# Modulation sums shared between VectorE and GpSimd, and the first block's stages on one calendar of row blocks

## What is computed

```python
def first_block(x, ...):
    h = rms_norm(x, norm_gain)
    proj = einsum('bsd,dc->bsc', h, w_in)                    # 1024 x 10240
    sb_q, sb_k, sb_v, sb_g, r_q, r_k, r_v, r_g, m_sb, m_ret = split(proj)
    out_a = stick_breaking_attention(rms_norm(sb_q), rms_norm(sb_k), sb_v) * silu(sb_g)   # 8 heads of 128
    out_b = rms_norm(chunkwise_retention(rotary(r_q), rotary(r_k), r_v)) * silu(r_g)      # 4 heads of 256
    merged = sigmoid(m_sb + b0) * (out_a @ w_branch_sb) + sigmoid(m_ret + b1) * (out_b @ w_branch_ret)
    return x + merged @ w_out

def second_block(x, c, ...):
    mod = silu(c) @ w_ada + b_ada            # 1024 x 6144, one row: shifts, scales and gates
    sh1, sc1, gt1, sh2, sc2, gt2 = split(mod, 6)
    h = rms_norm(x, norm_mix) * (1 + sc1) + sh1
    x = x + gt1 * token_mixer(h, ...)        # latent attention and an RWKV-7 branch
    h = rms_norm(x, norm_ffn) * (1 + sc2) + sh2
    return x + gt2 * peer_ffn(h, ...)        # 16384 experts
```

## Time and profile before

| | us |
|---|---|
| median of 3 runs | 1748.14 |
| lowest, highest | 1744.11, 1757.19 |
| the profiled execution, its own time | 1747.92 |
| its span in the trace | 1746.6 |
| TensorE busy | 1639.4 (94%) |
| VectorE busy | 889.7 (51%) |
| GpSimd busy | 415.9 (24%) |
| mean granted TensorE clock | 0.969 of full |

### The profile page before, as it was taken

One profiled execution on the slowest core, in us unless ns is written; L12 is line 12 of the kernel. 1 busy time (PEld: TensorE's weight loads), 2 busy tenths in 40 slices (PEclk: granted clock), 3 DMA queues, 4 the chain that ended last, 5 costly groups with the idle time before them and its releaser, 6 DMA issues.

```text
span 1746.6 us, 24304 instructions
## 1 busy us (share of the span) xinstructions
PE 1639.4 (94%) x9529; PEld 1215.1 (70%) x9529; DVE 889.7 (51%) x1838; ACT 545.1 (31%) x929; POOL 415.9 (24%) x273
## 2 busy tenths in 40 slices
PE   6998999999989996788889999999999999999998
PEld 2333554554445544754779999999999988888886
DVE  4775223331225326453458886333333477767776
ACT  1002333120112213111124344443334444545553
POOL 0000000000000021000048888888888200000000
PEclk9999999999999986989899999999999999999999
DMA  9993334233463473012346666666677477777776
GB/s 343 350 327 135 134 107 145 96 110 139 148 219 108 145 296 137 3 49 98 133 146 149 146 146 139 142 144 146 144 140 142 108 240 240 241 240 240 240 238 214
DMA packets 179572, 297.17 MB, mean 170 GB/s; under 512 B 48786, under 2 KB 94210, under 8 KB 179332
## 3 DMA queue, kind: packets, MB, share of 16 engines
q1 hardware_dynamic: 110704, 260.28, 43.6%
q0 software_dynamic: 36864, 0.15, 6.1%
q10 hardware_dynamic: 31892, 35.20, 5.9%
HBM read 276.55 MB, written 19.03 MB: 169 GB/s over the span
## 4 chain that ended last, share of the span: by engine, by line
PE 86%; DVE 7%; DMA 3%; issue 2%; ACT 2%; POOL 0%; ACTq 0%; SPq 0%; DVEq 0%; POOLq 0%
PE bank L456 26%; PE bank L869 14%; PE bank L867 14%; PE bank L871 13%; PE bank L879 6%; PE bank L849 3%; DVE ada_acc L964 3%; DMA slot<-in_w_in_dram 1%; PE bank L725 1%; PE bank L440 1%; DMA ada_b<-in_b_ada_dram 1%; DMA slot<-in_expert_down_dram 1%; PE bank L736 1%; PE bank L473 1%; PE bank L735 0%
## 5 line engine op out<-in xcount | busy, mean ns | idle before, releaser
L456 PE MATMUL bank<-slot,hT 128*128 128x512 f32 (+2 forms) x1088 | 479.6, 596 | 14.1 <-DMA slot<-in_w_in_dram 9.7
L1979 POOL DMA_INDIRECT c_dram<-gates,places x256 | 397.7, 1553 | 201.4 <-DVE gates L1512 123.7
L456 PEld LDWEIGHTS bank<-slot,hT 128*128 128x128 f32 x1088 | 206.7, 194 | 255.5 <-issue 244.3
L867 PE MATMUL bank<-hT_high,dT_high 128*128 128x256 f32 x1024 | 297.6, 291 | 0.0
L869 PE MATMUL bank<-hT_low,dT_high 128*128 128x256 f32 x1024 | 287.8, 281 | 0.0
L871 PE MATMUL bank<-hT_high,dT_low 128*128 128x256 f32 x1024 | 287.6, 281 | 0.0
L1424 DVE TENSOR_TENSOR dT_low<-bank,dT_high 128x512 fp32r<-128x512 f32 x256 | 165.0, 686 | 218.7 <-ACT dT_high L1900 217.5
L869 PE MATMUL bank<-up_low,A_high 128*128 128x512 f32 x512 | 202.2, 395 | 0.0
L867 PE MATMUL bank<-up_high,A_high 128*128 128x512 f32 x512 | 199.6, 390 | 0.4 <-DVE A_low L1424 0.4
L871 PE MATMUL bank<-up_high,A_low 128*128 128x512 f32 x512 | 198.8, 388 | 0.0
L867 PEld LDWEIGHTS bank<-hT_high,dT_high 128*128 128x128 f32 x1024 | 193.8, 189 | 0.0
(11 more groups left out here) (394 smaller groups left out, 1717.5 us busy)
## 6 DMA issues: line engine op xcount, KB each, us to landing
slot<-in_expert_down_dram SPq DMA_DIRECT2D x128, 512.0 KB
slot<-in_expert_up_dram SPq DMA_DIRECT2D x128, 512.0 KB, 3.4
slot<-in_w_in_dram SPq DMA_DIRECT2D x27, 2048.0 KB, 8.0
P<-in_w_ada_dram ACTq DMA_DIRECT2D x24, 1024.0 KB
c_dram<-zeros SPq DMA_DIRECT2D x1, 16384.0 KB, 50.7
slot<-c_dram SPq DMA_DIRECT2D x128, 128.0 KB, 3.3
slot<-in_w_out_dram SPq DMA_DIRECT2D x4, 2048.0 KB, 7.9
slot<-in_w_query_dram SPq DMA_DIRECT2D x4, 2048.0 KB, 8.1
```

Source lines behind the costliest of these rows:

```text
L456: m = pe.matmul(sums, lhsT=lhs[:, k, t * P:(t + 1) * P], rhs=w[:, k, :], start=(k == 0), stop=(k == w.shape[1] - 1))
L867: pe.matmul(o, lhsT=lhs_high.bitcast(F32R), rhs=rhs_high.bitcast(F32R), start=start, stop=False, skip_group_check=True)
L1979: g.indirect_dma_start(C_dram, bass.IndirectOffsetOnAxis(ap=places[:, x, k:k + 1], axis=0), gates[:, x, k:k + 1], None, compute_op=ALU.add ...
```

## The change

The 24 pieces are divided. VectorE sums pieces 0 to 11 as before, one at each of x = 2 to 13. GpSimd (`g_ada`) takes the other twelve: one product of all eight slices with the broadcast column `cs`, then additions of the halves (1024, 512 and 256 columns). Each engine has two weight buffers (RQ, RK for VectorE; M1, M2 for GpSimd). Two pieces share one row product of 512 columns, so that TensorE makes 12 of them, at x = 4, 5, 6, 8, 9, 10, 12, 13, 15, 16, 20 and 23, and biases and results are moved as 12 rows of 512. The loads of the pieces and biases move from ScalarE's queue to SyncE's, between the chunks; the constants are loaded by ScalarE's queue at once. One loop over x now orders every engine: a pair of attention heads starts at x = 14, 18, 22, 26 and takes six steps (normalise, transpose, scores, VectorE's part of the scores, running sums, weighting); the retention pairs start at x = 30 and 34; the square sums stand at x = 8 to 13 and the gates' silu at x = 17 and 33. ScalarE does each function for both heads of a pair in a row. `oaT` is transposed ahead of the block x = 39. The diff, cut:

```diff
--- before.py
+++ after.py
-    NP, AW, PIECES = 6, 256, ((0, 1), (2,), (3, 4), (5,))
-    ada_in = [sem(f"ada{p}_in") for p in range(NP)]
-    mod_out = [sem(f"mod_out{p}") for p in range(NP)]
-    ada_summed = sem("ada_summed")
+    AW = 256
+    SB, RET = [14 + 4 * i for i in range(4)], [30, 34]
+    ADA = 6 * D // AW // 2
+    ada_at = {2 + p: p for p in range(ADA)}
+    rows = [(4, 0, 0), (5, 1, 0), (6, 0, 1), (8, 0, 2), (9, 1, 1), (10, 0, 3), (12, 1, 2), (13, 0, 4), (15, 0, 5),
+            (16, 1, 3), (20, 1, 4), (23, 1, 5)]
+    row_at = {x: (n, who, m) for n, (x, who, m) in enumerate(rows)}
+    pool_load = {int((11.8 * (p - 1) + 4) / 6.9) + 1: p for p in range(2, ADA)}
+    row_of = {(who, m): n for n, (x, who, m) in enumerate(rows)}
+    ada_in = [[sem(f"ada{who}{j}_in") for j in range(2)] for who in ("v", "g")]
+    ada_b_in = [sem(f"ada_b{j}_in") for j in range(2)]
+    mod_out = [sem(f"mod_out{j}") for j in range(2)]
+    ada_summed = [sem("ada_summed_v"), sem("ada_summed_g")]
...
-    ada_w = [P1[:, p // 3, RQ + 2 * (p % 3):RQ + 2 * (p % 3) + 2, :].rearrange("p g d -> p (g d)")
-             .rearrange("p (k n) -> p k n", k=KT) for p in range(NP)]
-    ada_acc = [carve(f"ada_acc{p}", AW) for p in range(NP)]
-    ada_b = [carve(f"ada_b{p}", AW) for p in range(NP)]
-    mod_row = [carve(f"mod_row{p}", AW) for p in range(NP)]
+    ada_w = [[P1[:, j, at:at + 2, :].rearrange("p g d -> p (g d)").rearrange("p (k n) -> p k n", k=KT) for j in range(2)]
+             for at in (RQ, M1)]
...
+    ada_acc = [[gt[:, j * 2 * AW:(j + 1) * 2 * AW] for j in range(2)], [carve(f"ada_acc{j}", 2 * AW) for j in range(2)]]
+    cursor[0] = ret_at
+    ada_b = [carve(f"ada_b{j}", 2 * AW) for j in range(2)]
+    mod_row = [carve(f"mod_row{j}", 2 * AW) for j in range(2)]
...
+    def pe_ada_row(x):
+        if x in row_at:
+            n, who, m = row_at[x]
+            row = fill(("ada", n), 4 + n % 2)[0:1, :]
+            pe.wait_ge(ada_summed[who], 2 * m + 2)
+            pe.matmul(row, lhsT=col[:, 0:1], rhs=ada_acc[who][m % 2], start=True, stop=True).then_inc(filled(("ada", n)), 1)
...
+        for x in range(40):
+            for i in range(4):
...
+                step = {1: pe_sb_turn, 2: pe_sb_score, 4: pe_sb_keep, 5: pe_sb_weigh}.get(x - SB[i])
+                if step == pe_sb_turn and i == 0:
+                    pe.wait_ge(first_in, 16 * 9)
...
+                step = {2: pe_ret_turn, 3: pe_ret_score, 4: pe_ret_weigh}.get(x - RET[i])
...
+            if x == 39:
+                for j in range(2):
+                    clear(pe, ("sbo", 3, j))
+                pe_turn("oaT", tiles_of(P1[:, :, G_, :]))
+            pe_block(("in", x // 2), hT, x % 2)
+            pe_ada_row(x)
...
+    def v_ada_sum(x):
+        if x in ada_at:
+            p = ada_at[x]
+            m = p // 2
+            acc, w = ada_acc[0][m % 2][:, p % 2 * AW:(p % 2 + 1) * AW], ada_w[0][p % 2]
+            v.wait_ge(ada_in[0][p % 2], 16 * (m + 1))
+            if m > 1:
+                held(v, ("ada", row_of[0, m - 2]))
+            v_own.settle(v.tensor_scalar(acc, w[:, 0, :], cs[:, 0:1], None, ALU.mult))
             for k in range(1, KT):
-                m = v.scalar_tensor_tensor(ada_acc[p], ada_w[p][:, k, :], cs[:, k:k + 1], ada_acc[p], ALU.mult, ALU.add)
+                m = v.scalar_tensor_tensor(acc, w[:, k, :], cs[:, k:k + 1], acc, ALU.mult, ALU.add)
                 if k < KT - 1:
                     v_own.settle(m)
-            m.then_inc(ada_summed, 1)
-
-    def v_ada_row(i, q):
-        for p in PIECES[q]:
-            b = held(v, ("ada", i, p))
-            if i:
-                v.wait_ge(mod_out[p], 16 * i)
-            v.tensor_tensor(mod_row[p][0:1, :], b[0:1, 0:AW], ada_b[p][0:1, :], ALU.add).then_inc(emptied(("ada", i, p)), 1)
+            m.then_inc(ada_summed[0], 1)
+
+    def v_ada_row(x):
+        if x in row_at:
+            n, who, m = row_at[x]
+            b = held(v, ("ada", n))
+            v.wait_ge(ada_b_in[n % 2], 16 * (n // 2 + 1))
+            if n > 1:
+                v.wait_ge(mod_out[n % 2], 16 * (n // 2))
+            v.tensor_tensor(mod_row[n % 2][0:1, :], b[0:1, :], ada_b[n % 2][0:1, :], ALU.add).then_inc(emptied(("ada", n)), 1)
+
...
+        for x in range(40):
+            v_ada_row(x - 1)
+            for i in range(4):
+                q = x - SB[i]
+                step = {0: v_sb_norm, 1: v_sb_turn, 3: v_sb_score, 4: v_sb_keep, 5: v_sb_weigh}.get(q)
+                if step == v_sb_weigh and i == 0:
+                    v.wait_ge(sb_gated, 1)
                 if step:
                     step(i, 0)
...
+            v_ada_sum(x)
+            if x in (9, 10):
+                v_sb_sums(x - 9)
+            if x == 13:
+                v_sb_roots()
...
+            if x == 39:
+                v_turn("oaT", by_tile(oaT, KT), 4)
+            if x % 2 == 0:
+                c = x // 2
+                v_take(("in", c, 0, 0), P1c[:, 0, c * CW:(c + 1) * CW])
...
+    def a_sb_score(i):
+        for j in range(2):
+            z = held(a, ("sbz", i, j))
+            m = a.activation(sb_e[j], z[:, 0:3 * P], ACT.Abs)
+        a_own.settle(m)
+        for j in range(2):
+            m = a.activation(sb_e[j], sb_e[j], ACT.Exp, scale=-1.0)
+        a_own.settle(m)
+        for j in range(2):
+            a.activation(sb_e[j], sb_e[j], ACT.Ln, bias=col[:, 0:1]).then_inc(sb_softplus, 1)
...
+            if x == 1:
+                a_first_loads()
+            if x == 8:
+                a_sb_squares()
+            if x == 11:
+                a.wait_ge(sb_summed, 1)
+                a_root(stat[:, 0:32], stat[:, 0:32], SB_D, 1, sb_rooted)
...
+            if x == 36:
+                a_mod_loads()
+            if x == 39:
+                a_turn("oaT", by_tile(oaT, KT), 4)
+            a_ada_store(x - 2)
+            if x % 2:
+                c = x // 2
+                a_take(("in", c, 0, 1), P1c[:, 1, c * CW:(c + 1) * CW])
...
+    def g_ada():
+        g.wait_ge(silu_done, 1)
+        for p in range(ADA):
+            m = p // 2
+            acc, w = ada_acc[1][m % 2][:, p % 2 * AW:(p % 2 + 1) * AW], ada_w[1][p % 2]
+            g.wait_ge(ada_in[1][p % 2], 16 * (m + 1))
+            g_own.settle(g.tensor_tensor(w, w, cs.unsqueeze(2).broadcast_to([P, KT, AW]), ALU.mult))
+            for k in (4, 2):
+                g_own.settle(g.tensor_tensor(w[:, 0:k, :], w[:, 0:k, :], w[:, k:2 * k, :], ALU.add))
+            if m > 1:
+                held(g, ("ada", row_of[1, m - 2]))
+            g.tensor_tensor(acc, w[:, 0, :], w[:, 1, :], ALU.add).then_inc(ada_summed[1], 1)
...
+    def s_ada(who, p):
+        m, at = p // 2, AW * (ADA * who + p)
+        if p > 1:
+            sp.wait_ge(ada_summed[who], p - 1)
+        sp.dma_start(ada_w[who][p % 2], w_ada[:, at:at + AW].rearrange("(k p) n -> p k n", p=P)).then_inc(ada_in[who][p % 2], 16)
+    def s_ada_b(n):
+        x, who, m = rows[n]
+        at = 2 * AW * (6 * who + m)
+        if n > 1:
+            clear(sp, ("ada", n - 2))
+        sp.dma_start(ada_b[n % 2][0:1, :], I["b_ada_2"][:, at:at + 2 * AW]).then_inc(ada_b_in[n % 2], 16)
...
+                for x in (2 * i - 4, 2 * i - 3):
+                    if x - 1 in row_at and row_at[x - 1][0] + 2 < len(rows):
+                        s_ada_b(row_at[x - 1][0] + 2)
+                    if x in ada_at and ada_at[x] + 2 < ADA:
+                        s_ada(0, ada_at[x] + 2)
+                    if x in pool_load:
+                        s_ada(1, pool_load[x])
                 held(sp, chunk_end[chunks[i - 2][0]])
             sp.dma_start(chunk_view(name), w[:, c0:c0 + n].rearrange("(k p) n -> p k n", p=P)).then_inc(chunk_in[i % 2], 16)
+            if i == 0:
+                s_ada(1, 0)
+            if i == 1:
+                s_ada(0, 0)
+                s_ada(1, 1)
+                s_ada(0, 1)
+                for n in range(2):
+                    s_ada_b(n)
```

More of the change, by code:

```diff
@@ L547, in pe_first_block @@
                     step(i, 1)
[L548 to L552, removed]
+            for i in range(2):
+                step = {2: pe_ret_turn, 3: pe_ret_score, 4: pe_ret_weigh}.get(x - RET[i])
                 if step:
@@ L1073, in v_first_block @@
                     step(i, 1)
-                if q % 2 == 0:
-                    c = 16 + 2 * i + q // 2
-                    v_take(("in", c, 0, 0), P1c[:, 0, c * CW:(c + 1) * CW])
+            for i in range(2):
+                q = x - RET[i]
+                if q == 0 and i == 0:
+                    clear(v, ("in", 11, 0, 1))
+                if q in (0, 1):
+                    v_ret_rotate(i, q)
+                step = {2: v_ret_turn, 3: v_ret_score}.get(q)
+                if step:
+                    step(i, 0)
+                    step(i, 1)
+            v_ada_sum(x)
[3 more added lines that the diff above has]
+                v_sb_roots()
+            if x == 37:
+                v.wait_ge(merge_in, 32)
+                v.wait_ge(ret_gated, 1)
```

(39 more changed lines are left out.)

120 lines of the change are left out of this document (35 added, 85 removed).

## The result

| | before | after |
|---|---|---|
| median, us | 1750.04 | 1727.34 |
| lowest to highest | 1744.11 to 1757.19 | 1725.55 to 1732.51 |
| ratio, 95% interval | | 0.9873, 0.9829 to 0.9917 |
| profiled execution, span | 1746.6 | 1726.4 |
| first attention turn (T) | | 139.82 |

The kernel is 1.3% faster; 1728 was forecast. The kernel before had a median of 1750.04 in this comparison, so the gain is 22.7 us by the medians, where 20.1 was forecast. The part that the change touches ends 22.3 us earlier. So T and the start of the branch blocks are the sharper measures here.

What follows compares the result with a forecast made beforehand. TensorE was taken as the bound, with VectorE's sums second in the first 16 steps. T 140 plus 213.9 plus 2 gave 356 against 375.65, 19.7 less, so 1747.9 became 1728 us; range 1708 to 1750.

Steps and rivals of the forecast that it cites:

- The forecast of T: Start of the first attention turn, before block 15: 140 us, the middle of 133 (partly hidden) and 147 (none hidden).
- the hold-ups: VectorE's additions before T, blocked by about 6.5 GpSimd pieces on the shared SBUF port: 52 us.
- VectorE's lateness: At T, VectorE's sums, slowed by GpSimd's port use, come after TensorE could be ready: T 140 against 128.7.
- SyncE's order: Rival, SyncE's queue: chunk loads stand behind loads waiting for sums; T 151, 8.7 us gained, 1740 us; chance 0.2.
- TensorE alone: TensorE's own work without waits for other engines: T at 128.7, end at 342.5, 33.1 us earlier.
- no blocking: Rival, sums before T: no blocking that matters, only TensorE binds; 1714.8 us; chance 0.2.
- After T: TensorE from T to the first branch block: 25 blocks, products, four rows, oaT and the transpose, 213.9 us.
- late GpSimd pieces: Around x = 14 to 21, four such pieces delay normalisations and masks: 2 us added.
- The slower rival: Sums before T: VectorE gets one instruction per GpSimd instruction, GpSimd always supplied; T 182, 20 us lost, 1768; chance 0.1.
- Edits costed at nothing: ScalarE's grouping, six steps per pair, moved square sums and silus, GpSimd's later work, bias loads: no time gained or lost.
- the 355.9 of the sum: Start of the first branch block: T 140 plus 213.9 plus 2, given as 356 against 375.65 before.
- Two rivals: SyncE's order (1740 us, chance 0.2) and the slower rival (1768 us, chance 0.1).

Runs made afterwards that it cites:

- taking the port away: The changed kernel with GpSimd's product and additions left out, its 256 sums per piece only set to zero: 1713.5 us, ratio 0.9781 to the kernel before.
- The run with memsets: The changed kernel with GpSimd's product and additions replaced by memsets over the same buffers: 1718.3 us, ratio 0.9831 to the kernel before.

## Why the prediction was right

- **The forecast of T.** 140 was forecast as the middle of 133 and 147, 139.82 measured. The parts: VectorE's first piece at 32, measured 33.4; GpSimd's piece 8.0, measured 8.16 (22.09 to 30.25) for the first, with a product of 3.60; the hold-ups, 52 less about half of the 14.7 that could be hidden, so 45, measured 38.9 on the additions and 3.2 on the tensor_scalars (7.3 against 12 x 0.34). The inner terms missed by more than the sum: seven GpSimd pieces and not 6.5 fell between VectorE's first piece and T (from 36.17 to 134.5), 57.6 us of port instead of 52, and 15 of these were hidden instead of 7. The two misses cancelled, and the two ends were no more than bounds, so a hit within 0.2 us is partly luck.
- **What stood last at T was mixed.** I named VectorE's lateness; SyncE's order was a rival. In the trace TensorE waits for nothing of VectorE's before T, but for chunk 7 (5.4 us, and 2.6 of clock), whose load stood behind a sum. VectorE's first normalisation ended at 139.7, so that it bound at nearly the same moment. The experiments say how they belong together: taking the port away removes both (129.3), changing the order alone removes the wait for the chunk and makes VectorE later still (156.2). The root was the port; the rival's mechanism was its messenger. (Its time in the prediction should read 1739: 8.7 off 1747.9.) Its price of T = 151 was too high: it assumed a block of VectorE's additions that pass one by one in every round, but between its first and its eighth piece GpSimd waited 45 us for loads, and additions ran free then.
- **TensorE alone.** 128.7 was forecast for T; 129.3, 129.1 and 128.6 were measured once nothing blocked. The rival "no blocking" had 1714.8; the kernel with PSUM sums took 1714.6 and 1714.7. The row product was 0.95 as taken, block 0 started at 14.83 where I took 14.1.
- **After T.** 213.9 forecast, 213.5 measured (139.82 to 353.35). The 2 us that I added for late GpSimd pieces did not appear.
- **The slower rival** needed GpSimd always supplied. It got its pieces through the same queue and waited for them, as argued, and T never neared 162.
- **Edits costed at nothing** cost nothing that shows: no wait at the retention's turn, at the running sums or for a silu.

The end was off by 0.7 us in the median, and that is luck: the branch blocks began 2.6 us earlier than the 355.9 of the sum, mostly by the 2 us too many after T, and the part behind took 2.1 us longer than before.

Of 33 us that TensorE alone could have given, the change kept 22 in the trace. Of the 11 lost, 10 come from the port (7.4 of chunk waits and 2.6 of clock after them) and 0.7 from the later start of block 0.

The Trainium skill's rule (SBUF — State Buffer, "Who interferes with whom") was weighed beside the earlier trace rows. It goes further than that row did: it says that a VectorE instruction with two SBUF inputs contends with a GpSimd instruction that reads SBUF and not with one that only writes it. The run with memsets agrees, 485 ns throughout. It also says that a tensor_scalar in a two-port mode contends either way; the 760 ns beside memsets agree, if it ran in that mode here, which the trace doesn't show. For the product of 2048 the rows were nearer than the 4.5 us of the Trainium skill (GPSIMD Engine Reference, "Performance versus the Vector engine"), which is for an addition of two tensors: 3.60 here for a product with a broadcast operand.

## What to carry to other kernels

Before work is given to GpSimd beside VectorE, look at what VectorE runs at that moment: if its instructions read two SBUF tensors and GpSimd's read SBUF too, the two engines took turns in these traces, one instruction each, and a chain of short ones was stretched to the length of GpSimd's. Moving the running operand to an idle PSUM bank removed this for 5 ns per addition and 136 per tensor_scalar, and was worth 0.7% here. Leaving everything on VectorE was no worse than the half on GpSimd, so that is the first thing to try. A queue whose loads wait for sums passes such a delay on to all that stands behind, so look for the root before you reorder: here the reordering alone lost the whole gain.

## What was not expected of the hardware

- Two rivals assumed that one instruction of VectorE passes per instruction of GpSimd. It was as strict as that: in the stretch shown, four instructions of GpSimd (3.78, two of 3.81 together, 0.79) let through exactly four additions (3.72, 2.46, 1.38, 0.84), though each addition could begin some 0.03 us after the end of the one before.
- GpSimd hardly suffers: its product took 3.78 on average against 3.61 beside the PSUM sums, its whole piece 8.22 against 8.01. VectorE's additions took 0.947 against 0.485. The loss is on the side with the short instructions.
- A GpSimd memset of 2048 columns took 1.81 us and one of 512 took 0.53, and left two-input additions alone.
